# Expert weights in 8 KB runs per partition, with token features and hidden columns permuted to match

## The reference

```python
z = rmsnorm(h, ffn_norm)                              # (1040, 1024)
# router: softmax over 4 groups, the best group is taken; in it the best 2 of 8 experts
# 32 experts in all, each token goes to 2 of them
def expert_block(xb, e):                              # xb: rows of z
    return (silu(xb @ w_gate[e]) * (xb @ w_up[e])) @ w_down[e]
# w_gate, w_up: (32, 1024, 512); w_down: (32, 512, 1024)
h = h + weighted sum of the two experts' rows
out = rmsnorm(h, final_norm)
```

## Time and profile before

| | |
|---|---|
| time, median of 3 runs | 1486.88 us (1485.43 to 1486.91) |
| span of the profiled execution | 1484.6 us; no other time of this execution is given |
| PE busy | 1231.9 us (83%), 6174 instructions |
| DVE busy | 860.2 us (58%) |
| ACT busy | 737.3 us (50%) |
| DMA packets | 137804, 285.04 MB |
| mean granted TensorE clock | 0.946 |

### The profile page before, as it was taken

The page is one execution under the profiler, slowest core; times in us unless marked ns, Lnnn a source line. Parts: engine busy times, 40 slices in busy tenths (PEclk is TensorE's granted clock), DMA queues, the critical chain, the costliest instruction groups (busy, mean ns, idle before and its releaser), DMA issues. The chain is left out here.

```text
span 1484.6 us, 18548 instructions
## 1 busy us (share of the span) xinstructions
PE 1231.9 (83%) x6174; PEld 931.1 (63%) x6174; DVE 860.2 (58%) x952; ACT 737.3 (50%) x851; POOL 79.3 (5%) x140
## 2 busy tenths in 40 slices
PE   3799999999999996999258988889888889888810
PEld 3587687678768764887136666666666666666600
DVE  4334534553453454432757777777778777777725
ACT  5334434343434434322056676666766666767512
POOL 0000000000000000110010000000000000000033
PEclk9999999999999998999579999999999999999965
DMA  4211010111101011653469999999999999999546
GB/s 129 49 54 43 30 42 0 43 43 28 43 28 42 12 31 61 230 168 119 184 213 345 353 334 344 347 369 332 345 334 357 352 342 343 339 346 352 189 147 218
DMA packets 137804, 285.04 MB, mean 192 GB/s; under 512 B 12280, under 2 KB 38904, under 8 KB 137776
## 3 DMA queue, kind: packets, MB, share of 16 engines
q1 hardware_dynamic: 125728, 242.09, 46.4%
q0 software_dynamic: 8464, 30.02, 6.7%
q10 hardware_dynamic: 3584, 12.58, 2.2%
HBM read 255.01 MB, written 29.66 MB: 192 GB/s over the span
## 5 line engine op out<-in xcount | busy, mean ns | idle before, releaser
L1408 DVE TENSOR_TENSOR m_wl<-raw,m_wh 128x2048 fp32r<-128x2048 f32 x192 | 429.5, 2288 | 114.4 <-ACT m_wh L1350 114.4
L1350 ACT ACTIVATE m_wh<-raw 128x2048 fp32r<-128x2048 f32 x192 | 360.2, 1911 | 81.5 <-PE m_py L277 31.5
L275 PE MATMUL m_py<-m_wh,m_hh 128*96 128x512 f32 x256 | 108.7, 424 | 58.7 <-DVE m_hl L1428 58.7
L289 PE MATMUL a_pj<-zh,a_wh 128*128 128x348 f32 (+1 forms) x432 | 112.1, 359 | 0.0
L289 PE MATMUL a_pj<-zl,a_wh 128*128 128x348 f32 (+1 forms) x432 | 111.8, 358 | 0.0
L289 PE MATMUL a_pj<-zh,a_wl 128*128 128x348 f32 (+1 forms) x432 | 110.7, 355 | 0.0
L276 PE MATMUL m_py<-m_wl,m_hh 128*96 128x512 f32 x256 | 105.1, 411 | 0.0
L277 PE MATMUL m_py<-m_wh,m_hl 128*96 128x512 f32 x256 | 104.2, 407 | 0.0
L275 PE MATMUL m_pg<-m_wh,m_xh 128*96 128x512 f32 x256 | 101.4, 396 | 1.9 <-DVE m_xl L1412 1.9
L277 PE MATMUL m_pg<-m_wh,m_xl 128*96 128x512 f32 x256 | 101.8, 398 | 0.0
L276 PE MATMUL m_pg<-m_wl,m_xh 128*96 128x512 f32 x256 | 101.3, 396 | 0.0
(11 more groups left out here) (259 smaller groups left out, 2094.9 us busy)
## 6 DMA issues: line engine op xcount, KB each, us to landing
raw<-in_w_gate_dram SPq DMA_DIRECT2D x64, 1024.0 KB, 7.1
raw<-in_w_up_dram SPq DMA_DIRECT2D x64, 1024.0 KB, 7.7
raw<-in_w_down_dram SPq DMA_DIRECT2D x64, 1024.0 KB, 8.0
a_raw<-in_w_in_dram SPq DMA_DIRECT2D x26, 512.0 KB, 3.9
yrows<-m_ys ACTq DMA_DIRECT2D x32, 384.0 KB, 6.8
yrows<-o_blank POOLq DMA_DIRECT2D x22, 384.0 KB, 4.5
a_cb<-negcum SPq DMA_DIRECT2D x8, 520.0 KB, 3.9
n_x<-in_x_dram SPq DMA_DIRECT2D x8, 512.0 KB, 3.3
```

The lines of the kernel that those rows point to most:

```text
L275: nc.tensor.matmul(out, xh, wh, start=first, stop=False)
L289: mm = nc.tensor.matmul(out, w[:, k, 0:m], z[:, k, at:at + n], start=n_pass == 0, stop=n_pass == PASSES - 1)
L1350: nc.scalar.activation(wh[s][:], raw[j][:], ACT.Copy).then_inc(S["w_hi"], 1)
L1408: nc.vector.tensor_tensor(wl[s][:], raw[j][:], wh[s][:].bitcast(F32), ALU.subtract).then_inc(S["w_lo"], 1)
```

## The change

It redistributes rows. Before, partition p of unit j holds rows p, p + 128, ... of half a matrix, each a run of 2 KB in HBM (gate, up: 512 values) or 4 KB (down: 1024 values). After, partition p holds consecutive rows: of gate and up, rows 8p to 8p + 3 in the first unit and 8p + 4 to 8p + 7 in the second; of down, rows 4p, 4p + 1 and 4p + 2, 4p + 3. Each is one run of 8 KB. To match, `z2` is written so that column k x 128 + p holds feature 8p + k (`by_lane`, `by_tile`), the router weights are loaded in the same order, and `hid` is written so that column k x 128 + p holds hidden column 4p + k. The writes of `z2` and `hid` thus step 512 bytes from one value to the next. Numbers, order and waits of instructions are as before.

```diff
@@ -865,6 +865,14 @@
             return buf[:].rearrange("p (k t) -> p k t", k=KD)
 
 
+
+        def by_tile(ap):
+            return ap.rearrange("q b (l k) -> q b l k", k=KD)
+
+        def by_lane(buf):
+            return buf[:].rearrange("q (k b l) -> q b l k", k=KD, b=KD)
+
+
         ROUNDS = NT // 2
 
         with nc.Block() as block:
@@ -881,8 +889,8 @@
                 for k in range(SLOTS, KD):
                     weights(k)
                 sp.dma_start(gain[:], ffn_norm[0, :].partition_broadcast(P)).then_inc(small_in, 16)
-                sp.dma_start(wr[:, :, 0:NG], w_rg[0].rearrange("(k p) n -> p k n", p=P)).then_inc(small_in, 16)
-                sp.dma_start(wr[:, :, NG:NR], w_re[0].rearrange("(k p) n -> p k n", p=P)).then_inc(small_in, 16)
+                sp.dma_start(wr[:, :, 0:NG], w_rg[0].rearrange("(p k) n -> p k n", p=P)).then_inc(small_in, 16)
+                sp.dma_start(wr[:, :, NG:NR], w_re[0].rearrange("(p k) n -> p k n", p=P)).then_inc(small_in, 16)
                 sp.dma_start(br[:, 0:NG], b_rg[0, :].partition_broadcast(P)).then_inc(small_in, 16)
                 sp.dma_start(br[:, NG:NR], b_re[0, :].partition_broadcast(P)).then_inc(small_in, 16)
 
@@ -965,8 +973,8 @@
                     dve.wait_ge(x_in[n], i * 16 + 16)
                     nc.vector.tensor_tensor(mix_tile(i, n), three(xt[n]), three(ph[n]), ALU.add).then_inc(S["h2_done"], 1)
                     dve.wait_ge(S["squared"], i * 2 + (n + 1))
-                    nc.vector.scalar_tensor_tensor(out=three(z2[n]), in0=mix_tile(i, n), scalar=rs[:, n:n + 1],
-                                                   in1=three(gain), op0=ALU.mult, op1=ALU.mult).then_inc(S["z2_done"], 1)
+                    nc.vector.scalar_tensor_tensor(out=by_lane(z2[n]), in0=by_tile(mix_tile(i, n)), scalar=rs[:, n:n + 1],
+                                                   in1=by_tile(three(gain)), op0=ALU.mult, op1=ALU.mult).then_inc(S["z2_done"], 1)
                     if ahead:
                         mix_low(i, n + 2)
                     dve.wait_ge(S["logits"], i * 2 + (n + 3))
@@ -1223,11 +1231,10 @@
 
 def unit(raw, j, e, w_gate, w_up, w_down):
 
-    if j < 4:
-        n, part = DE, (w_gate, w_up)[j // 2][0, bass.ds(e, 1), (j % 2) * D // 2:(j % 2 + 1) * D // 2, :]
-    else:
-        n, part = D, w_down[0, bass.ds(e, 1), (j % 2) * DE // 2:(j % 2 + 1) * DE // 2, :]
-    return raw[:].rearrange("p (k n) -> p k n", n=n), part.rearrange("o (k p) n -> p (o k) n", p=P)
+    n, w = (DE, (w_gate, w_up)[j // 2]) if j < 4 else (D, w_down)
+    half = UNIT // n
+    rows = w[0, bass.ds(e, 1), :, :].rearrange("o (p k) n -> p (o k) n", p=P)
+    return raw[:].rearrange("p (k n) -> p k n", n=n), rows[:, (j % 2) * half:(j % 2 + 1) * half, :]
 
 
 def experts(c, nc, tag, pairs, block0, w_gate, w_up, w_down):
@@ -1422,7 +1429,9 @@
                         dve.wait_ge(S["silu_done"], N + 1)
                         dve.wait_ge(S["unit_used"], products(N, UP))
                         dve.wait_ge(S["h_turned"], N + 1)
-                        nc.vector.tensor_tensor(hid[:], act_g[:], pu[:], ALU.mult).then_inc(S["h_done"], 1)
+                        nc.vector.tensor_tensor(hid[:].rearrange("q (k p) -> q p k", p=P),
+                                                act_g[:].rearrange("q (p k) -> q p k", p=P),
+                                                pu[:].rearrange("q (p k) -> q p k", p=P), ALU.mult).then_inc(S["h_done"], 1)
                         x_low(N + 1, 1 - u)
                         dve.wait_ge(S["h_hi"], N + 1)
                         nc.vector.tensor_tensor(hl[:], phid[:, 0:DE // P * BLK], hh[:].bitcast(F32), ALU.subtract).then_inc(S["h_lo"], 1)
```

## The result

The changed kernel takes 1491.52 us (median of 14 runs, 1489.43 to 1495.86), the kernel before, run beside it, 1486.79 us (14 runs, 1484.96 to 1489.51). The ratio is 1.0036, 95% interval 1.0027 to 1.0045: 4.0 to 6.7 us slower. The forecast was 1487, no change, with a range that reached to 1497. The range held the time; the likeliest case was the wrong one.

The account below looks back on a forecast made before the run. PE's own work plus one hand-over was taken to fill each expert's period, with room for transfers. All parts of the change were put at 0, so 1486.9 + 0 gave 1487 us; 8-in-10 range 1484.5 to 1497.

Parts of the forecast that it names:

- Step 1: Weight transfers in 8 KB runs: some 9% less engine time, worth 0 because of 5 us to spare.
- Step 2: Router weights loaded in the new order: 1024 runs of 4 and of 32 values each way, as before; 0.
- Step 3: Stepped write of hid in the experts: same rate taken, 0; first 0.6 us covered; double 0 to 3 us, triple 16.
- Step 4: Stepped write of z2 in the output projection: same rate taken, 0; 2.4 us cover; double +6.3 us, triple +15.
- rival A: Single-element writes of z2 and hid cost double, about 1494 us, chance 0.28; triple, 1518 us, chance 0.05.
- Rival D: Number of clock falls behind the m_hl gap changes: none 1476 us, one per expert 1520; chance fewer 0.04, more 0.03.

Follow-up runs that it names:

- e3: Kernel before with only the weight transfers changed to 8 KB runs, matching permutations left out (result not the reference's): 1486.7 us, ratio to before 0.9998.
- e6: Kernel before with one exchange in the experts: ACT's m_hh ahead of m_xh, DVE's m_hl ahead of m_xl: 1462.5 us, ratio to before 0.9836.
- e4: Changed kernel with z2 and hid written in order and the permutation made by stepped reads of PE's transposes: 1490.5 us, ratio to before 1.0021.
- e8: Changed kernel with one extra 0.68 us DVE operation just ahead of the hidden one: 1499.7 us, ratio to before 1.0088.
- e2: Changed kernel without its first half: only hidden columns and w_down permuted, z2, router weights, gate and up as before: 1487.6 us, ratio to before 1.0001.
- e7: Changed kernel with the exchange of e6 (m_hh ahead of m_xh, m_hl ahead of m_xl): 1489.8 us, ratio to before 1.0019.
- e1: Changed kernel without its second half: z2, router weights, gate and up permuted, hidden tile and w_down as before: 1491.9 us, ratio to before 1.0030.
- e10: The kernel of e6 unchanged, run again on the same chip as e9: 1463.5 us, ratio to before 0.9840.
- e5: Kernel before with fourteen forms of a 128x1024 VectorE product in front, differing in steps: 1.25 us flat, 1.92 to 2.02 us for writes stepping 4 values or more.
- e9: e6 plus w_down in 8 KB runs and hidden columns permuted by stepped PSUM reads of ACT and DVE: 1463.3 us, ratio to before 0.9837.

## Why the prediction was right or wrong

**What bounds the kernel: right.** PE's own work and one hand-over fill the period, transfers have room. e3 shows it for the transfers: fewer packets, a lower share, the same time. e6 shows it for the hand-over: 0.60 us less in it is 0.60 us less in the period.

**Step 1, transfers, 0: right** (e3, 0.9998). That the engine time saved would be some 9% was an estimate from q10; it was 3% (q1).

**Step 2, router weights, 0: right as far as shown.** The edit was not run alone, but e4 contains it, with a projection that is 0.35 us longer than before; 0.2 of it are the transposes with stepped reads.

**Step 3, the hidden operation: value wrong, result right.** The same rate was taken; it was 1.53 times the time. The cover had been worked out as 0.6 us, and e8 measured 0.60; +0.36 us stayed inside (e2, 1.0001). That the wait for `m_hl` stays 1.85 us did not come true: it gave up the 0.36 us and fell to 1.49. e6 and e7 show that the cover is `m_xh` and `m_xl`.

**Step 4, `z2`: this is the step that failed.** "Value taken for (3) and (4): the same rate" gave 0, and the operation grew by 0.78 us. The rule of the step was sound: 8 x 0.78 - 2.4 = 3.8 us against 4.3 measured (e1 minus before). Most of the half microsecond that it missed is in the transposes themselves, which take 1.09 instead of 1.03 to 1.06 us when they start late, 0.4 us in seven tiles. The forecast's own line for a write half as slow again said +2; the write was 1.6 times as slow in all and 1.7 times a column. At 2.07 us it lay past the 1.95 from which the forecast said that rival A decides. So the mechanism of rival A came true, at a smaller size than its double.

**Why the wrong value.** It came from "the nearest rows", operations cut into runs of 128 values. Those rows write four values to each 16 bytes, the new writes one, so they were near in shape and far in what counts. The text said "nearest is not very near", and then gave the case half of the chance. The page of the Trainium skill spoke of one access to each line, without naming writes, no row contradicted it, and rival A, for which it spoke, was the nearer one: it said 1494, the time was 1491.5. Between a row that doesn't show the thing and a rule that bears on it, the rule deserved more than 0.33.

**Rival D, the clock**, had 0.07 and did not happen: 8 falls before and after in the traced runs. But the experiments show that it was no idle thought: 0, 2, 5, 6, 8 and 12 falls in traced runs whose periods differ by under 1 us.

## What to carry to other kernels

A permutation of 4-byte values belongs where PSUM is read, not where SBUF is written or read: on DVE a step of 16 bytes or more in SBUF cost 1.5 to 1.6 times, two reads at 512 bytes 1.8 times, and a step of 16 or 512 bytes in the read of PSUM nothing. Before a transfer is made cheaper, look whether anyone waits for it: here the change bought 3% of DMA time that nobody waited for and paid with DVE time just where PE waits. And ask of each hand-over what stands ahead of the operation that the busy engine needs; the exchange of two pairs of operations gave 1.6% (e6, e10).

## What was not expected of the hardware

- DVE: 1.25 us for 1024 columns in order or in steps of 8 bytes, 1.92 to 2.02 us from 16 to 2048 bytes, no dependence on the distance for writes; two reads at 512 bytes 2.30 us (e5).
- DVE and ACT read PSUM in steps of 16 bytes, and DVE in steps of 512, at full rate (e5, e9).
- PE pays for stepped reads in transposes of 96 rows: 1.02 instead of 0.82 us for eight, with weight loads of 204 instead of 140 ns. In transposes of 128 rows the loads grew too, 193 instead of 140 ns, but eight took hardly longer, 1.05 to 1.12 instead of 1.03 to 1.06 us (e4).
- SyncE's issue of a weight transfer shortened from 0.37 to 0.33 us with the longer runs.
- The granted clock falls to 0.50 for over 3 us behind some hand-overs, 1.3 to 1.6 us each. Runs of one kernel differ in it: the mean clock of e9 was 0.947 to 0.953, its times 1465.0 to 1456.2 us, and only the fastest is known to have had no fall. Kernels differ in it too, and a longer period can go with fewer falls (e8) or with more (e7). A comparison of single runs carries this, up to 9 us in one kernel.
